# Attention sums differences of values by its own scan, and the second weight pair runs as four blocks

## The reference

```
proj = einsum('bsd,de->bse', rmsnorm(x, norm_g), w_in)       # sb_q, sb_k, sb_v, sb_z, hg_q, hg_f, hg_i, hg_z, gates
z = einsum('bhqd,bhkd->bhqk', qb, kf) * scale
causal = key_pos[None, :] < q_pos[:, None]
log_not = where(causal, log_sigmoid(-z), 0.0)
survive = cumsum(log_not, axis=3, reverse=True) - log_not
w = exp(where(causal, log_sigmoid(z) + survive, -inf))
out = einsum('bhqk,bhkd->bhqd', w, vf)
gates = sigmoid(gate_logits + b_gate)                        # y = gate_sb * u_sb + gate_hg * u_hg, then w_out
```

## Time and profile before

| | |
|---|---|
| median of 3 runs | 1380.04 us (1379.36 to 1381.21) |
| the profiled execution | 1382.87 us, span 1381.1 us, mean granted clock 0.990 |
| PE busy | 1340.9 us (97% of the span) |
| DVE busy | 944.4 us (68%) |
| ACT busy | 585.0 us (42%) |
| POOL busy | 724.6 us (52%) |
| chain that ended last | PE 83%, DVE 5%, POOL 3%, issue 2% |

### The profile page before, as it was taken

The page is one execution under the profiler, slowest core; times in us unless marked ns, Lnnn a source line. Parts: engine busy times, 40 slices in busy tenths (PEclk is TensorE's granted clock), DMA queues, the critical chain, the costliest instruction groups (busy, mean ns, idle before and its releaser), DMA issues.

```text
span 1381.1 us, 23094 instructions
## 1 busy us (share of the span) xinstructions
PE 1340.9 (97%) x8421; PEld 1115.3 (81%) x8421; DVE 944.4 (68%) x1075; ACT 585.0 (42%) x965; POOL 724.6 (52%) x484
## 2 busy tenths in 40 slices
PE   7989999999999999999999999999999989999998
PEld 6778788788888878878878888887877868788886
DVE  5868877877967987787796797888544634545323
ACT  7645356256346435625634633653444411101121
POOL 5965554744665556565466456554678622223210
PEclk9989999999999999999999999999999999999999
DMA  5111311121112211121111211115452475433502
GB/s 184 31 46 31 93 61 32 63 77 46 63 31 67 63 56 61 32 90 64 31 63 59 64 63 32 62 40 145 167 192 98 143 238 191 134 92 122 199 26 103
DMA packets 128221, 119.41 MB, mean 86 GB/s; under 512 B 3920, under 2 KB 110464, under 8 KB 128128
## 3 DMA queue, kind: packets, MB, share of 16 engines
q1 hardware_dynamic: 118912, 92.84, 21.2%
q10 hardware_dynamic: 9216, 25.17, 5.2%
HBM read 88.63 MB, written 29.36 MB: 85 GB/s over the span
## 4 chain that ended last, share of the span: by engine, by line
PE 83%; DVE 5%; POOL 3%; issue 2%; ACT 1%; DMA 1%; DVEq 0%; ACTq 0%; POOLq 0%
PE banks L1695 46%; PE banks L2005 11%; PE banks L2027 6%; PE banks L1780 5%; PE banks L1756 4%; PE banks L1770 2%; POOL b_lo L638 1%; PE banks L1839 1%; POOL b_sum L638 1%; DVE hk L1176 1%; PE banks L1814 1%; PE banks L1739 1%; PE banks L1841 1%; PE banks L1834 1%; PE banks L1820 1%
## 5 line engine op out<-in xcount | busy, mean ns | idle before, releaser
L1695 PE MATMUL banks<-a_hi,b_hi 128*128 128x512 f32 x1092 | 444.5, 407 | 9.0 <-DVE k_raw L1176 4.3
L1695 PE MATMUL banks<-a_hi,b_lo 128*128 128x512 f32 x1092 | 428.5, 392 | 0.0
L1695 PE MATMUL banks<-a_lo,b_hi 128*128 128x512 f32 x1092 | 427.4, 391 | 0.0
L638 POOL TENSOR_TENSOR b_lo<-w_raw,b_hi 128x512 fp32r<-128x512 f32 x106 | 162.2, 1540 | 222.6 <-ACT b_hi L747 222.6
L638 POOL TENSOR_TENSOR b_lo<-b_sum,b_hi 128x512 fp32r<-128x512 f32 x117 | 176.0, 1504 | 156.0 <-ACT b_hi L747 156.0
L1695 PEld LDWEIGHTS banks<-a_hi,b_hi 128*128 128x128 f32 x1092 | 205.9, 189 | 51.3 <-issue 6.8
L1695 PEld LDWEIGHTS banks<-a_hi,b_lo 128*128 128x128 f32 x1092 | 205.7, 188 | 45.5
L1695 PEld LDWEIGHTS banks<-a_lo,b_hi 128*128 128x128 f32 x1092 | 206.4, 189 | 37.1
L1307 DVE TENSOR_TENSOR_SCAN kappa<-kappa 128x128 f32<-128x128 f32 (+3 forms) x64 | 90.9, 1421 | 86.6 <-ACT kappa L924 86.6
L747 ACT ACTIVATE b_hi<-b_sum 128x512 fp32r<-128x512 f32 x117 | 73.9, 632 | 156.1 <-POOL b_sum L638 151.2
L731 POOL TENSOR_TENSOR w_lo<-w_raw,w_hi 128x1024 fp32r<-128x1024 f32 x20 | 54.9, 2747 | 143.8 <-ACT w_hi L747 143.8
(11 more groups left out here) (218 smaller groups left out, 2584.5 us busy)
## 6 DMA issues: line engine op xcount, KB each, us to landing
w_raw<-in_w_in SPq DMA_DIRECT2D x72, 512.0 KB, 5.0
gate_d<-gate_out SPq DMA_DIRECT2D x16, 512.0 KB, 3.3
gate_in<-gate_d ACTq DMA_DIRECT2D x32, 256.0 KB, 2.7
x_tok<-in_x SPq DMA_DIRECT2D x8, 512.0 KB, 5.7
z_d<-z_out SPq DMA_DIRECT2D x8, 512.0 KB, 2.6
hz_d<-z_out SPq DMA_DIRECT2D x8, 512.0 KB, 2.6
osb_d<-o_sb SPq DMA_DIRECT2D x8, 512.0 KB, 7.1
ohg_d<-hq SPq DMA_DIRECT2D x8, 512.0 KB, 2.7
```

What stands on the lines that cost most here:

```text
L638: return nc.gpsimd.tensor_tensor(dst, a, b, op)
L1695: last = mm(bank, w[:, s, k, :], t[s][:, k, :], start=opens and k == 0 and z == 0, stop=k == QUAD - 1 and z == 2, skip_group_check=not opens)
```

## The change

The parts, in words:

1. Attention: ACT makes only kappa. DVE scans it in place, and nothing else (`weigh`). PE turns the scan itself. ACT writes 1 - x for each turned block, not x. In place of the values PE turns v_diff, their differences over tokens, which DVE makes in a new function `differences`: one subtraction of 128x1023 and one copy of 128x1. It stands behind C21 of the values, ahead of the last three reciprocals, and PE's `turn_values` waits for it (`v_made`).
2. The second pair is multiplied as four blocks (96 matmuls in place of 84) in the order (1,0), (1,1), (0,0), (0,1). The weights need four splits and no sums; ACT copies the four results out of PSUM; DVE's additions L1522 to L1542 go, and k_lo and q_lo come before the last two low parts of the activation sums. PE waits for s_ready 4 ahead of the third pair.
3. The small rows are loaded from ACT's queue and no longer from SP's.
4. `fetch_gate(0)` is issued ahead of `finish_gate` of the last pair, and no longer behind the first fetch of the HGRN2 branch.
5. Tiles are laid out anew: beta goes, pair_hi, pair_raw and pair_lo take its place, quad_hi that of kappa1, and three waits (w_done, wtr_done twice) go with it.

```diff
@@ sync
-                    sp.wait_ge(raw_sum, 4 * n)
-                    sp.wait_ge(w_ready, PRODUCTS + SECOND_SPLIT_ORDER.index(P3) + 1)
+                    sp.wait_ge(w_ready, 2 * PRODUCTS)
             load_x(0)
             load_x(1)
-            load_small(0, KT, norm_g[0].rearrange("(k p) -> k p", p=P))
-            (four more)
@@ gpsimd
+            def second_low(rows, panel, made):
+                pool.wait_ge(hi_ready, PRODUCTS + made)
+                hi, lo = second_weights(rows, panel)
+                tt(lo..., raw_block(rows, panel), hi..., ALU.subtract).then_inc(w_ready, 1 if made < 4 else 4)
             pool.wait_ge(w_loaded, 32)
-            second_split(P1, raw_block(0, 0))
...
+            for i, (rows, panel) in enumerate(FIRST_BLOCKS[:3]):
+                second_low(rows, panel, i + 1)
             pool.wait_ge(a_ready, KT)
             tt(flat(raw_a12), flat(a_hi[P2]).bitcast(F32), flat(a_lo[P2]).bitcast(F32), ALU.add).then_inc(a_back, 1)
...
+            second_low(*FIRST_BLOCKS[3], 4)
@@ scalar
+            def load_small(row, n, src):
+                act.dma_start(small_rows[row:row + n, :], src).then_inc(small_in, 16)
+            load_small(0, KT, norm_g[0].rearrange("(k p) -> k p", p=P))
+            (four more)
             norm_tiles(0, 4)
...
+            def take_second(tokens, panel, done):
+                act.wait_ge(product_done, PRODUCTS + done)
+                return copy(halfs((turn_in, z_out)[panel], tokens), banks[:, SECOND_BLOCKS[tokens, panel], :])
+            take_second(1, 0, 1).then_inc(p1_copied, 2)
+            act.wait_ge(qk_split, 2)
+            take_second(1, 1, 2).then_inc(block_taken, 5)
+            sum_high(P3, raw_s4, s4_made)
             act.wait_ge(lb_step, 1)
             nc.scalar.activation(lb[:, :], lb_low, ACT.Sigmoid).then_inc(lb_step, 1)
-            for t in SPLIT_ORDER[2:-1]:
+            for t in SPLIT_ORDER[2:4]:
                 split(2, t)
+            take_second(0, 0, 3).then_inc(first_taken, 2)
+            for t in SPLIT_ORDER[4:-1]:
+                split(2, t)
+            take_second(0, 1, PRODUCTS).then_inc(block_taken, 5)
...
-                copy(wT[:, first:first + n, :].rearrange("p t e -> p (t e)"), turned[:, 0:n * P]).then_inc(wT_ready, 1)
+                nc.scalar.activation(wT[:, first:first + n, :].rearrange("p t e -> p (t e)"), turned[:, 0:n * P],
+                                     ACT.Identity, scale=-1.0, bias=1.0).then_inc(wT_ready, 1)
...
-                nc.scalar.activation(keys(beta[j % 2]), score, ACT.Sigmoid, scale=SB_SCALE)
                 nc.scalar.activation(keys(kappa[j % 2]), score, ACT.Sigmoid, scale=-SB_SCALE).then_inc(sig_done, 1)
...
+            fetch_gate(0)
+            finish_gate(N_GATE_PAIRS - 1)
+            for i in range(2):
+                act.wait_ge(gate_stored[i], 16 * N_GATE_PAIRS)
             act.wait_ge(product_done, PRODUCTS * N_PAIRS)
             fetch_ohg(0)
-            fetch_gate(0)
             fetch_ohg(1)
@@ vector
             def weigh(h, j):
...
-                v.tensor_tensor_scan(back, back, back, 1.0, ALU.mult, ALU.min).then_inc(scan_done, 1)
-                dve.wait_ge(scan_done, 8 * h + j + 1)
-                tt(b[:, S - n:S], b[:, S - n:S], k[:, S - n + 1:S + 1], ALU.mult).then_inc(w_done, 1)
+                v.tensor_tensor_scan(back, back, back, 1.0, ALU.mult, ALU.min).then_inc(w_done, 1)
+            def differences(h):
+                dve.wait_ge(block_taken, 5 * (4 * h + 1) + 5)
+                dve.wait_ge(first_taken, 4 * h + 2)
+                tt(v_diff[:, 1:S], turn_in[:, 1:S], turn_in[:, 0:S - 1], ALU.subtract).then_inc(v_made, 1)
+                v.tensor_copy(v_diff[:, 0:1], turn_in[:, 0:1]).then_inc(v_made, 1)
...
                 take_c21(pairs[1], n + 1, h)
+                if qk:
+                    differences(h)
                 if attend:
                     for i in range(1, 4):
                         invert(a, i)
@@ tensor
             def turn_values(h):
-                pe.wait_ge(block_taken, 5 * (4 * h + 1) + 5)
-                pe.wait_ge(first_taken, 4 * h + 2)
+                pe.wait_ge(v_made, 2 * h + 2)
...
+            for i, ((tokens, panel), bank) in enumerate(SECOND_BLOCKS.items()):
+                if i == 0:
+                    pe.wait_ge(w_ready, PRODUCTS + 2)
+                    pe.wait_ge(s3_made, QUAD)
+                if i == 1:
+                    pe.wait_ge(w_ready, 2 * PRODUCTS)
+                if i == 2:
+                    pe.wait_ge(s1_made, QUAD)
+                for k in range(KT):
+                    last = first_block(tokens, panel, k, second_weights, bank)
+                last.then_inc(product_done, 1 if i < 3 else 4)
+            pe.wait_ge(block_taken, 5)
+            pe.wait_ge(s_ready, 4)
```

More of the change, by code:

```diff
@@ L29 @@
 IDENT_MADE = 2
-EARLIER_MADE = 8
+EARLIER_MADE = 6
 CONSTANTS = EARLIER_MADE + 2 * MASKED
@@ L199, in build @@
         i_tok = place("i_tok", block_at(10), [NT, P])
-        beta = [place("beta0", block_at(11), [S]), place("beta1", block_at(13), [S])]
-        kappa = [place("kappa0", block_at(12), [S + 1]), place("kappa1", block_at(14), [S + 1])]
+        kappa = [place("kappa0", block_at(12), [S]), place("kappa1", block_at(14), [S])]
+        v_diff = place("v_diff", block_at(11), [S])
         wT = place("wT", block_at(15), [NT, P])
-        quad_hi = place("quad_hi", block_at(11), [S], F32R)
+        quad_hi = place("quad_hi", block_at(14), [S], F32R)
         qk_hi = place("qk_hi", block_at(12), [S], F32R)
@@ L444, in first_weights, with second_weights @@
             return (b_hi[:, P6, :, :], b_lo[:, P6, :, :]) if (rows, panel) == (0, 1) else first_b[rows, panel]
+        def second_weights(rows, panel):
+            s = {(0, 0): P2, (1, 0): P3, (0, 1): P4}.get((rows, panel))
+            return first_b[0, 0] if s is None else (b_hi[:, s, :, :], b_lo[:, s, :, :])
         def pair_bank(n, s):
@@ L1111, in _ @@
                         split_panel(0, w_hi[:, 0, :, :])
-            finish_gate(N_GATE_PAIRS - 1)
-            for i in range(2):
-                act.wait_ge(gate_stored[i], 16 * N_GATE_PAIRS)
             def fetch_gate(t):
@@ L1243, in _ @@
             low_sum(P6, raw_s2, 2)
+            dve.wait_ge(k_hi_ready, 1)
+            tt(k_lo[:, :], first_out[:, 2:4, :].rearrange("p a n -> p (a n)"), k_hi[:, :].bitcast(F32), ALU.subtract).then_inc(qk_split, 1)
+            dve.wait_ge(q_hi_ready, 1)
+            tt(q_lo[:, :], first_out[:, 0:2, :].rearrange("p a n -> p (a n)"), q_hi[:, :].bitcast(F32), ALU.subtract).then_inc(qk_split, 1)
             low_sum(P5, raw_s1, 3)
@@ L1733, in tile, with turn_tokens @@
                 return t[:, n * P:(n + 1) * P]
-            def turn_tokens():
+            def turn_tokens(src):
                 for bank, first in ((attended, 0), (turned, 4)):
                     for i in range(4):
-                        last = nc.tensor.transpose(tile(bank, i), tile(turn_in, first + i), ident[:, :])
+                        last = nc.tensor.transpose(tile(bank, i), tile(src, first + i), ident[:, :])
                     last.then_inc(tok_done, 1)
@@ L1769, in turn @@
                 for i in range(4 * part, min(4 * part + 4, j + 1)):
-                    last = nc.tensor.transpose(tile(turned, i % 4), beta[j % 2][:, S - n + i * P:S - n + (i + 1) * P], ident[:, :])
+                    last = nc.tensor.transpose(tile(turned, i % 4), kappa[j % 2][:, S - n + i * P:S - n + (i + 1) * P], ident[:, :])
                 last.then_inc(wtr_done, 1)
@@ L1905, in _, with first_block @@
                         last.then_inc(xT_done, 1)
-            def first_block(rows, panel, k, closes=True):
-                tokens, bank = rows, banks[:, panel, :]
-                hi, lo = first_weights(k // QUAD, panel)
+            def first_block(tokens, panel, k, weights=first_weights, bank=None):
+                bank = banks[:, panel if bank is None else bank, :]
+                hi, lo = weights(k // QUAD, panel)
                 if tokens == 0:
```

127 lines of the change are left out of this document (31 added, 96 removed).

## The result

The changed kernel took 1385.45 us (median of 6, 1383.92 to 1386.63) against 1381.03 for the kernel before in the same runs: a ratio of 1.0036, 95% interval 1.0026 to 1.0046. It is slower by 4.4 us. The forecast was 1378.1. Its profiled execution has a span of 1384.0 us against 1381.1.

The account below looks back on a forecast made before the run. The prediction took PE, busy 97% of the span, as the bound. Its terms, -6.1 second pair, +7.5 attention, -3.3 first gate and 0 start, summed to -1.9, carried from the 1380.04 median to 1378.1 us; range 1369.5 to 1386.

Parts of the forecast that it names:

- Second pair: Head 0, four blocks: DVE's additions go, PE waits 2.4 us for the values and resumes at 72.85; -6.1 us.
- Attention: Seven heads: v_diff ahead of the reciprocals makes PE's first turn 1.07 us later in each; +7.5 us.
- The narrow copy: The 128x1 copy of v_diff on DVE: taken at 0.15 us, not held by POOL's operation.
- Rival 2: Each head: the 128x1 copy waits behind POOL's low part, chain 2.65 us later; +8.0, or 1388.0 us; chance 0.13.
- Rows 8: Profile rows before the change: beside POOL, a 128x1 reciprocal took 0.16 us, a 128x8 TENSOR_SCALAR 1.10.
- First gate: Branch panel 1: earlier gate fetch leaves the low part late, 2.05 us back plus 1.2 of half clock; -3.3 us.
- Start: Kernel start: loading the small rows from ACT's queue changes nothing; 0, within 0.4 us.
- Rival 1: Attention heads: no wait per head, since PE's first turn has slack or the chain closes up; 1370.6 us, chance 0.27.
- Rival 3: Second pair: result copies stand behind t6 and splits, PE waits 6 us at half clock; returns 2.5, 1381.7 us; chance 0.10.

Follow-up runs that it names:

- a_split_first: a_pad50 with ScalarE's high part of branch panel 1 put ahead of the wait for the gate's stores and the fetches; 1367.03 us, ratio 0.9908.
- a_pad50: The changed kernel with 50 more instructions on TensorE ahead of everything, waits that already hold; 1371.64 us against 1381.1, ratio 0.994.
- a_pad200: The changed kernel with 200 more instructions on TensorE ahead of everything, waits that already hold; 1385.99 us against 1379.88.

## Why the prediction was wrong

What failed is a term that was not in the sum. The part "the second pair" priced twelve added matmuls at 2.8 us of PE and at nothing else. They are also 24 more instructions ahead of a loop, and that moved the loop's start from 1119 to 1137, 10 instead of 28 instructions in front of a boundary of the instruction pieces. The stretch from the loop's first matmul to the first one across the boundary took 2.4 to 3.4 us in every round that stopped at the fifth matmul; twelve matmuls nearly fill it before, four do not after. That is +12.2 of stops (11.2 of marked idle) and 1.6 of half clock; by the medians the stops cost 13.8. The rows to see it by lay in the trace of before, as 0.18 us of "issue" at the twelfth matmul behind a jump back and as 79 packets of instructions, and I read neither. The Trainium skill ("Runtime: NRT & Kernel Launch", section "Instruction fetch mechanics") says that instructions come in blocks of 256 and that a taken jump to a block that isn't held makes the engine wait for a fetch. The packets of 16.3 KB agree with it, and so do the two packets behind each jump in the kernels with 79 or 80 of them. The same section of the Trainium skill gives TensorE room for 2048 instructions. Here a loop of 1721 was kept where it lay in seven pieces and not where it lay in eight, so being shorter than 2048 was not enough, and the measurement decides.

Step by step, against the forecast's own terms:

- **Second pair, -6.1.** The mechanism was right, the size too small. PE resumed at 71.40, where I had 72.85, since POOL's t6 ended at 64.8 and not at 66.0; the wait was 1.4 and not 2.4. The subtraction lasted 2.27 beside a POOL operation that already ran, as I had allowed for. The half clock that I weighed at 0.7 did not come. Up to k_raw of head 1 it is -10.1 in the trace (0.8 of it a shorter wait for k_raw), and the four blocks alone, padded, measured -10.9. One sum of mine was off by 0.3: ACT's six pieces of 0.6 behind 66.0 end at 69.6, not 69.3.
- **Attention, +7.5.** Its reasons held to a tenth: subtraction 1.23, copy 0.15, reciprocals behind them, idle of 0.85 to 0.88 seven times against 1.07 forecast. The idle is then 6.1 in seven heads, not 7.5, and what PE lost was a little less still: 4.6 in six heads between the two kernels without fetches. Alone, the part cost 2.8 by the medians, and where the rest of that difference lies is open.
- **The narrow copy.** Taken at 0.15; all eight took 0.14 to 0.15, beside POOL's operation too. Rival 2 did not happen. Rows 8 had decided that rightly. Of the two pages of the Trainium skill that the prediction weighs, the eight copies bear out "VectorE: DVE Perf Modes", section "What auto-detection actually checks".
- **First gate, -3.3.** -1.5 in the wait (5.78 to 4.25) and -1.2 behind it. ACT's high part came only 0.3 sooner behind the first fetch and not 0.95, since the fourth fetch's issue took 1.36 us. That the low part is the next to be late was right, and a_split_first showed it.
- **Start, 0.** Right, within a scatter of the first projection matmul of 1.7 us.
- **The rivals.** Rival 1 gave 1370.6, close to a_pad50's 1371.6, but for a wrong reason: it said there is no wait per head. Rival 3 (the values 6 us late) did not happen.

Without the stops the terms that I did have were off by 7.6 in the other direction: a_pad50 is 9.5 below before, where I had 1.9. So the sign would have been right and the size not. The range did hold the result, by an accident of two errors of opposite sign.

## What to carry to other kernels

On the engine that bounds, instructions ahead of a long loop can cost far more, or less, than their own time, since they move the loop against the pieces in which the program is fetched. Count what a change adds before the loop, and look at the first microseconds behind each jump back for idle that is marked "issue", and at the count of instruction packets. If they move with the change, shift the loop by padding before judging the change itself. And when a part delays one thing in a chain, first look whether the thing PE waits for must stand behind it at all: moving one scan by one place gave back all that the delay had cost.

## What the runs showed of the hardware

- TensorE fetches its program in pieces of 16.3 KB. A loop of 1721 instructions was fetched once for all rounds (26 packets) or anew in each round (79 or 80), by where it started. With pieces of 256 instructions, which fits all fourteen kernels, that is seven pieces against eight.
- In the kernels that fetched anew, a packet started 0.9 to 1.6 us behind each jump back and a second one 3.0 to 3.9 us after that. The first matmul across the next boundary started 2.4 to 3.4 us behind the loop's first one (6.4 to 7.4 us behind the jump itself) in all rounds with a stop at the fifth matmul. Where the boundary was 66 instructions away (a_pad200) no stop was seen.
- A stop of 1.4 to 3.1 us in dense matmuls was sometimes followed by half clock for about eight matmuls (1.6 us) and sometimes not; in the changed kernel by one of six.
- 400 waits that hold already, 200 instructions, took PE 21.6 us at the start, 0.108 us an instruction; 16.2 of it was delay, since PE has 6.7 us of idle there.
- A copy of 128x1 took 0.15 us beside POOL, eight times. A subtraction of 128x1023 took 1.23 us in seven heads, where POOL's operation began only while it ran, and 2.27 in the one where POOL's already ran.
